# Seven-product projection of a second block: block sums through DRAM, roots inverted on 128x16, pooled rotation one group later

## The reference

```python
h = rms_norm(x, norm_w[l]) * (1.0 + scale[:, None, :]) + shift[:, None, :]
proj = jnp.einsum('bsd,de->bse', h, w_in[l])            # 1024 -> 2888
u_pool, g_pool, q, k, v, g_attn, qi, ki, wi = jnp.split(proj, split_points, axis=-1)
pool_out = pool_mixer(u_pool, w_pool[l], pool_scale[l]) * jax.nn.silu(g_pool)
q = rope(rms_norm(q.reshape(B, S, N_HEADS, HEAD_DIM), q_norm_w[l]), pos)
k = rope(rms_norm(k.reshape(B, S, N_KV_HEADS, HEAD_DIM), k_norm_w[l]), pos)
qi = rope(qi.reshape(B, S, N_IDX_HEADS, IDX_DIM), pos)
```

## Time and profile before

| what | value |
|---|---|
| median of 3 runs | 3106.57 us (3103.05 to 3109.3) |
| the profiled execution's own time | 3103.51 us |
| its span in the trace | 3101.7 us |
| mean granted clock of PE | 0.977 of full speed |
| busy, share of the span | PE 94%, DVE 78%, ACT 56%, POOL 17% |
| out_b, 1599 to 1738 us | 139 us, PE busy 121.8 |
| rotate, 1738 to 2248 us | 510 us, 24 groups |

### The profile page before, as it was taken

One profiled execution on the slowest core, in us unless ns is written; L12 is line 12 of the kernel. 1 busy time (PEld: TensorE's weight loads), 2 busy tenths in 40 slices (PEclk: granted clock), 3 DMA queues, 4 the chain that ended last, 5 costly groups with the idle time before them and its releaser, 6 DMA issues. The chain is left out here.

```text
span 3101.7 us, 49546 instructions
## 1 busy us (share of the span) xinstructions
PE 2916.2 (94%) x17248; PEld 2326.3 (75%) x17248; DVE 2428.9 (78%) x3533; ACT 1746.5 (56%) x3207; POOL 522.3 (17%) x791
## 2 busy tenths in 40 slices
PE   6999999999999999999998898899977899999899
PEld 5888888888878886777777677677755677777687
DVE  8888887766676758889878799799768898888553
ACT  5343422232454537777767654555478899888510
POOL 2000000000000001000114333343212333243100
PEclk8999999999999999999999999999989999999999
DMA  4434422257755433111135544544471111111774
GB/s 123 124 106 128 153 68 68 68 184 258 220 153 168 144 114 102 36 37 39 46 99 192 169 150 129 171 126 155 143 146 45 25 32 28 26 39 39 166 220 140
DMA packets 414557, 355.22 MB, mean 115 GB/s; under 512 B 100738, under 2 KB 362882, under 8 KB 411876
## 3 DMA queue, kind: packets, MB, share of 16 engines
q1 hardware_dynamic: 412500, 347.79, 38.2%
q0 software_dynamic: 1088, 3.93, 0.7%
q10 hardware_dynamic: 720, 0.31, 0.1%
HBM read 229.13 MB, written 112.87 MB: 110 GB/s over the span
## 5 line engine op out<-in xcount | busy, mean ns | idle before, releaser
L349 ACT ACTIVATE s_mx_w_hi<-s_mx_raw 128x512 fp32r<-128x512 f32 x224 | 138.5, 628 | 310.3 <-PE p_oa_acc L705 238.0
L705 PE MATMUL p_oa_acc<-s_h_a_hi,s_mx_w_hi 128*128 128x512 f32 x744 | 291.4, 392 | 8.8 <-DVE s_h_a_lo L448 7.1
L705 PE MATMUL p_oa_acc<-s_h_a_hi,s_mx_w_lo 128*128 128x512 f32 x744 | 290.3, 390 | 0.0
L705 PE MATMUL p_oa_acc<-s_h_a_lo,s_mx_w_hi 128*128 128x512 f32 x744 | 290.2, 390 | 0.0
L2151 PE MATMUL p_pr_ps<-s_pr_x_hi,s_pr_w_hi 128*128 128x512 f32 x588 | 233.1, 396 | 13.9 <-DVE s_pr_w_lo L2116 9.0
L1825 DVE TENSOR_TENSOR_SCAN s_st_prod<-s_st_soft,s_st_prod 128x512 f32<-128x512 f32 x192 | 234.8, 1269 | 8.2 <-ACT s_st_soft L1752 7.5
L2151 PE MATMUL p_pr_ps<-s_pr_x_lo,s_pr_w_hi 128*128 128x512 f32 x588 | 231.2, 393 | 0.0
L2151 PE MATMUL p_pr_ps<-s_pr_x_hi,s_pr_w_lo 128*128 128x512 f32 x588 | 231.0, 393 | 0.0
L1752 ACT ACTIVATE s_st_soft<-p_st_z 128x512 f32<-128x512 f32 (+3 forms) x320 | 153.4, 533 | 108.5 <-PE p_st_z L1878 107.7
L4243 PE MATMUL p_sa_turn<-s_ident,s_sa_arg 128*128 128x128 f32 x1088 | 164.8, 287 | 42.3 <-ACT s_sa_prob L3841 23.0
L491 DVE TENSOR_TENSOR s_mx_w_lo<-s_mx_raw,s_mx_w_hi 128x512 fp32r<-128x512 f32 x224 | 153.3, 685 | 53.6 <-ACT s_mx_w_hi L349 52.1
(11 more groups left out here) (489 smaller groups left out, 7890.3 us busy)
## 6 DMA issues: line engine op xcount, KB each, us to landing
s_mx_raw<-in_w_in_a SPq DMA_DIRECT2D x128, 256.0 KB, 3.8
s_pb_ada<-in_w_ada SPq DMA_DIRECT2D x16, 768.0 KB, 7.2
s_pr_w_a<-in_w_in SPq DMA_DIRECT2D x44, 256.0 KB, 3.2
s_pr_w_raw<-in_w_in SPq DMA_DIRECT2D x44, 256.0 KB, 3.3
d_rot_hi<-s_pr_rot SPq DMA_DIRECT2D x18, 512.0 KB, 2.7
d_y_t<-s_mx_y SPq DMA_DIRECT2D x16, 512.0 KB, 5.4
s_oa_y_raw<-d_y_t SPq DMA_DIRECT2D x16, 512.0 KB, 6.9
s_oa_x<-in_x SPq DMA_DIRECT2D x16, 512.0 KB, 4.9
```

What stands on the lines that cost most here:

```text
L705: ins = nc.tensor.matmul(bank, w[:, m, k, :], a[:, m, k, :], start=(k == 0 and n == 0), stop=(k == KH - 1 and n == 2))
```

## The change

1. **Block sums.** `sum` leaves rotate. In project, at steps 8 to 14, SP loads the raw blocks of the 11 groups that have them (`load_blocks`, four of 256 KB each), POOL makes the four sums (`sum_blocks`, 44 operations), and SP stores them to DRAM one step later (`store_blocks`, `d_w_sums`). rotate then loads seven blocks per group where it loaded four, each straight to the place of its low part, for both halves of the sequence.
2. **Roots.** The four reciprocals of 128x256 are replaced: the 64 rows of a head hold the same root, so two DMAs gather one row of each head into 128x16 (`gather_roots`), one reciprocal inverts that, a DMA stores 8 KB to DRAM and two broadcast it to 128x1024 (`spread_inverse`). `times_inverse`, `low_turned`, `take_high` and the stores of a norm group come one group later.
3. **Pooled turn.** The index query of a pool group is multiplied, added, split and stored one group later, in the group after the next norm group's first half; `mix` moves from behind the fourth product to behind the fifth.
4. **finish** (128x512) goes from POOL to DVE, ahead of `leave_c`.
5. **out_b.** The 14 gates go from POOL to DVE; the pieces of the factor are made one per step from 9 to 16, then 2, 1, 2, 1; the first whole group waits for the pieces of its own product only; two of the four last `store_late` go ahead of the A12 load.

The core of the diff (declarations, space and argument changes left out):

```diff
+    def load_blocks(self, sp, w_in, n):
+        j, of = n % 2, column_groups(0)[1 + n]
+        if n >= 2:
+            sp.wait_ge(self.blocks_out[j], 64 * (n // 2))
...
+    def store_blocks(self, sp, w_sums, n):
+        sp.wait_ge(self.blocks_summed, 4 * n + 4)
...
+    BLOCKS_AT = {8: (0, 1), 9: (2,), 10: (3, 4), 11: (5,), 12: (6, 7), 13: (8,), 14: (9, 10)}
...
+            for n in BLOCKS_AT.get(g - 1, ()):
+                proj.store_blocks(sp, w_sums, n)
+            for n in BLOCKS_AT.get(g, ()):
+                sp.wait_ge(late_lo, AHEAD)
+                proj.load_blocks(sp, w_next, n)
         next_space.load_first(sp, out_t, (upper_out, 16 * END), product, MULTS * END)
...
-    PIECES_AT = {9: 2, 10: 2, 11: 1, 12: 1, 13: 2, 14: 2, 15: 2, 16: 1, 17: 1}
+    PIECES_AT = {**{step: 1 for step in range(9, 17)}, 17: 2, 18: 1, 19: 2, 20: 1}
...
+        def gather_roots(g):
+            sp.wait_ge(rooted, norms_to(g) + 1)
...
+                sp.dma_start(roots[rows], wide[h * HD:h * HD + 1].rearrange("o (c n) -> o c n", n=pairs.ROOTS)).then_inc(roots_in, 16)
+        def store_inverse(g):
+            sp.wait_ge(roots_inverted, norms_to(g) + 1)
...
+            sp.dma_start(inverse_row.rearrange("h (c n) -> (h c) n", n=pairs.ROOTS), roots[:]).then_inc(inverse_out, 16)
+        def spread_inverse(g):
+            sp.wait_ge(inverse_out, 16 * (norms_to(g) + 1))
...
+                sp.dma_start(inverse[h * HD:h * HD + HD], inverse_row[h].partition_broadcast(HD)).then_inc(inverse_in, 16)
...
     def gpsimd(pool):
-        for g in range(1, N):
...
-                for n in range(3):
-                    pairs.sum(nc, pool, nxt, n)
-            if kinds[g] != "tail":
-                finish(g)
...
+        late_difference()
...
     def scalar(act):
+            norm, pool = older(g, "norm"), older(g, "pool")
...
+            if pool is not None:
+                take_high(pool)
+            if more and g:
+                pairs.split_hi(nc, act, nxt, S.A11_B11)
             if whole:
                 keep_u2(g)
...
-                if q == S.A12_B21 and kinds[was] == "pool":
+                if q == S.S3_T3 and kinds[was] == "pool":
                     mix(was)
```

More of the change, by code:

```diff
@@ L2741, in sync @@
                 load_late_half(0)
-            if g and kinds[was] != "gates":
+            if was_kind in ("norm", "tail"):
                 swap(was)
-            if nxt < N and nxt > 1 and kinds[nxt] != "tail":
-                for which in ("a21", "a22", "a11"):
-                    pairs.load(sp, nxt, which)
-            if g and kinds[was] == "tail":
+            if kinds[g] != "tail" and was_kind != "tail":
+                pairs.load(sp, g, S.A22_T4)
+            if more:
+                pairs.load(sp, nxt, S.A11_B11)
@@ L2748, in sync @@
+            if norm is not None:
+                store_rot(norm)
+            if was_kind == "tail":
                 store_tail(was)
-            if g and kinds[was] == "norm":
+            if was_kind == "norm":
                 store_plain(was, True, lower_out[was % 2])
-            if g and kinds[was] == "gates":
+            if was_kind == "gates":
                 store_plain(was, False, upper_out[was % 2])
                 store_plain(was, True, lower_out[was % 2])
+            if more:
+                pairs.load(sp, nxt, S.S1_T1)
@@ L2754, in sync @@
+            if norm is not None:
+                store_low(norm)
+            if was_kind == "norm":
+                gather_roots(was)
+            if pool is not None:
+                store_rot(pool)
+            if more:
+                pairs.load(sp, nxt, S.S2_T2)
+            if pool is not None:
+                store_low(pool)
+            if was_kind == "norm":
+                store_inverse(was)
             if g == LAST:
                 load_late_half(1)
-            if nxt < N and nxt > 1:
-                if kinds[nxt] == "tail":
-                    for h in range(2):
-                        pairs.load_tail(sp, nxt, h)
-                else:
-                    pairs.load(sp, nxt, "a12")
@@ L2762, in sync @@
-            if g and kinds[was] == "pool":
+                for h in range(2):
+                    pairs.load_tail(sp, nxt, h)
+            if more:
+                pairs.load(sp, nxt, S.A12_B21)
+            if was_kind == "norm":
+                spread_inverse(was)
+            if more:
+                pairs.load(sp, nxt, S.S3_T3)
+            if was_kind == "pool":
                 store_pooled(was)
-            if g and kinds[was] != "gates":
+                swap(was)
+            if was_kind == "tail":
@@ L2765, in sync @@
                 store_rot(was)
                 store_low(was)
+            if more:
+                pairs.load(sp, nxt, S.S4_B22)
+                if kinds[g] == "tail":
+                    pairs.load(sp, nxt, S.A22_T4)
             if g == N - 2:
@@ L2999, in scalar @@
                 late_high(2)
-            if was_kind == "norm":
-                take_high(was)
             if kinds[g] == "norm":
@@ L3219, in vector @@
                 late_low(0)
-            if more and g:
-                pairs.split_lo(nc, dve, nxt, S.S1_T1)
-            if was_kind == "norm":
-                invert(was, 3)
-                times_inverse(was)
-            if more and g:
-                pairs.split_lo(nc, dve, nxt, S.A11_B11)
-            if was_kind in ("pool", "tail"):
+            if more:
+                pairs.split_lo(nc, dve, nxt, S.S2_T2)
+            if was_kind == "tail":
                 low_turned(was)
```

362 lines of the change are left out of this document (183 added, 179 removed).

## The result

The changed kernel takes 3112.57 us (median of 12 runs, 3108.53 to 3119.61), the kernel before, run beside it, 3105.67 (12 runs, 3101.83 to 3112.42). The ratio is 1.0025, with a 95% interval of 1.0016 to 1.0033: a little **slower**, where 3076 was forecast. The profiled execution of the changed kernel took 3109.64, its span is 3107.6, so 5.9 over the span of before.

A forecast was written before the change was run, and what follows sets the result against it. PE sets rotate's pace, and most of its idleness is DVE's lateness, with DVE slowed beside POOL. Terms 11 + 8 + 10 + 3 - 2 = +30 us gave 3073.5, or 3076 on the median's footing; 8-in-10 range 3048 to 3102.

The forecast's parts named there:

- The bottleneck: In rotate, PE sets the pace and DVE, slowed beside POOL's sums, is late; 34.8 us lost in sixteen groups.
- the sixteen groups: Groups of norm and pool in rotate: 347.1 us instead of 358.25, gain +11, bounds +35 and -4.
- The odd groups: Eight rotate groups after a pool group: 20.8 us each, 166.4 together, 0.35 each over their floor.
- Out_b: Thirteen tiles before the tail: half of 15.5 lost us taken back, +8, bounds 0 and 13.
- the tail and first groups: Tail and first two groups, 69.4 us with 53.1 of work: gain +10, bounds 3 and 15.
- the middle: Four groups with the tail, 85.7 us, 1966.09 to 2051.75: gain +3, bounds 0 and 8.
- the stall at S3_T3: Eight groups after a norm group: PE waits for `keep_u2`, at least 1.4 us, taken as 2.0 each; 180.7 together.
- the 0.6 for the clock: Average loss from the lower clock after each S3_T3 stall in the eight groups after a norm group.
- Rival two: S3_T3 stall is 3 us with 1.5 for the lower clock each time: 195.9 for eight groups, 3091; chance 0.15.
- DVE's schedule: After a norm group: six operations end at 7.78 us, three more for the pool tile at 11.2; `keep_u2` done at 13.2.
- The ends, "-2": SP's queue at project's end and later stores at rotate's end cost 2 us, bounds 0 and -6.
- Rival three: Roots' store lands in 8.8 us, not 2.7, holding SP's queue: 3.3 lost in ten pairs, 3109; chance 0.09.

The follow-up runs named there:

- experiment 6: Kernel before with POOL's four sums per group replaced by memsets; only the rotation is read: last group starts at 2195.20 instead of 2229.37 us.
- experiment 8: Kernel before with parts 1 and 5, loads in order of products, A22 split later: 3077.62 us, ratio 0.9907.
- experiment 2: Changed kernel with A22's low part behind the older pool tile's three operations on DVE: 3106.49 us.
- experiment 3: Changed kernel with SP reordered: next phase's first loads before the last two block-sum stores, last group's plain stores before the norm tile's: 3116.26 us.
- experiment 1: Changed kernel with `keep_u2` ahead of the older pool tile's copy and A11's copy on ACT: 3112.00 us, ratio 1.0016.
- experiment 5: experiment 1 with the next group's loads ahead of pool-tile stores and the roots' store and spread on SP: 3095.11 us, ratio 0.9961.
- experiment 11: experiment 8, `mix` behind fifth product, `split_pooled` behind `keep_u2`; A11's low part, and in first half's last group A22's load and `keep_u3`, earlier: 3068.96 us, ratio 0.9875.

## Why the prediction was wrong

**The bottleneck and what its removal is worth: right.** DVE's lateness beside POOL held PE. With the sums gone and the orders kept the last group starts 32 us earlier (experiment 6), and the program with the sums from DRAM takes 3077.6 (experiment 8). That this lies next to the 3076 that was forecast for the whole change is chance: there the sixteen groups give 25.0 us where the forecast has 11, and the other stretches take 15.0 back. Low parts of 687 ns, `mix` at 2.1 us of waiting and PE at 80.00 in project came as forecast. The odd groups' sum of 166.4 us is the forecast's to the digit by luck: seven groups stand at 20.45 to 20.69, near their floor, and one, with the widest window of the first half, takes 22.77. Out_b gave 6.1 for 8, the tail and first groups 6.3 for 10, the middle 2.3 for 3, each inside its bounds.

**The step that failed is the stall at S3_T3, "8 x (19.99 + 2.0 + 0.6) = 180.7".** The place, the engine, the cause and the count were right; both sizes were not. The eight groups took 201.6, 25.2 each: the stall of 2.0 was 2.82 to 4.15 us, 3.24 in the mean, and the 0.6 for the clock was 1.97 (1.7 to 3.1 in seven groups; 0.3 in the one behind whose stall the granted clock stayed at 1.00). In the stretch from 1855.0 to 1858.5 the granted clock was 0.63. So the sixteen groups lost 10 us where 11 were to be gained, below the term's lower bound of -4; of the 36 us by which the forecast missed in the profiled executions, 21 are here. Rival two named 3 us and 1.5, and even that was short. Two things were missing from DVE's schedule, which I had taken from a group without a gate. The squares start at 2.45 us, not at 1.78, behind the table load. And A22's load, which in the kernel before was made a group earlier, is now issued behind the swaps of the same group, so that its low part holds cos back to 6.73 us; experiment 2 measured that piece, 12.8 us of the eight groups. With both, the pool tile's sum ends at 12.8 instead of 11.2, and `keep_u2` at 14.9 instead of 13.2. In the two groups without a gate the squares did start at 1.78, and the late loads of S4's sum and of A22 did the harm: the pool tile's sum ended at 13.9 and 14.0.

**The ends, "-2":** +2.3 ahead of out_b and +4.6 behind the last group, over the bound of 6. The queue order that I named explains a quarter of it at most (experiment 3). The cause of the 4.0 us within the selection, whose instructions are the same, stays open; over all these kernels but experiment 6, that stretch takes 847 to 855 us.

**Rival three** did not decide the time: in the changed kernel the spread was issued 1.6 to 3.2 us after the roots' store, as with the 2.7 that I took, and the odd groups paid nothing. But the mechanism is real, by other waits than the one it named. With `keep_u2` ahead (experiment 1) SP's queue takes the stall's place, at `keep_u3` and at `mix`, and with the loads moved ahead (experiment 5) the store's landing, then up to 4.5 us, and the spread's behind it hold DVE.

**What it comes to.** Parts 1 and 5 together give -29 us, part 4 nothing or a loss of a few, and parts 2 and 3, roots inverted through DRAM and tiles finished one group later, cost 30 to 35 as ordered; with the two orders of experiments 1 and 5, 17 of them come back. Reciprocals were worth 5 to 9 us by themselves, and in experiments 6, 8 and 11 the even groups stand at their floor with all of them. How the loss divides between parts 2 and 3, and the gain between parts 1 and 5, was not tried apart, nor were the small transfers tried on another queue than SP's.

## What to carry to other kernels

An engine that is busy 91% is worth relieving only where something waits for it: of two removals here, 52 us of DVE's own reciprocals gave 5 to 9 us, and 146 us of sums on POOL, for which PE waits in no row, gave some 30. In the best kernel (experiment 11) DVE is again busy 91.0 of the 100 us from 1800 on, and PE all of them. When a change also re-orders, lay out the new schedule for the worst group with every load's issue time in it, and ask what the in-order engine holds behind each new wait; a copy that empties a bank for PE belongs ahead of any copy that waits for a long chain. Try the parts apart: the gain of one can be hidden whole under the price of the others, as 29 us were here.

## What the runs showed of the hardware

POOL's memsets did not slow DVE: in experiment 6 POOL was still busy (16.7 of 100 us between 1800 and 1900), with low parts at 697 ns, against 687 in the changed kernel, where POOL stands still there. With POOL's sums, which read two operands, their mean was 917. In project, where the sums went, DVE's instructions in the window from 1040 to 1120 have a mean of 0.80 us (64.76 of 81) instead of 0.64 (48.72 of 76). The largest case is a single one in experiment 11, where POOL's subtraction of 128x2048 runs beside DVE's of the same shape:

```profile
1955.68 4.59 POOL L2821 TENSOR_TENSOR s_pr_x_raw<-s_pr_ahead,s_pr_ahead 128x2048 f32<-128x2048 f32 x1
```

```profile
1956.57 5.84 DVE L3153 TENSOR_TENSOR s_pr_x_raw<-s_pr_ahead,s_pr_x_raw 128x2048 f32<-128x2048 f32 x1 [4.84 <-DMA s_pr_x_raw<-d_rows_late]
1962.51 2.29 DVE L3158 TENSOR_TENSOR s_pr_x_raw<-s_pr_ahead,s_pr_x_raw 128x2048 f32<-128x2048 f32 x1
```

DVE's took 5.84 us there and 2.29 right after: it lost 3.55 of the 3.70 us in which both ran. In this kernel that loss is on DVE's way to the low parts of the late factors, behind which PE stands for 11.3 us ahead of the tail. The Trainium skill ("SBUF — State Buffer", section "Who interferes with whom") says that a DVE instruction with two SBUF inputs contends with a GpSimd instruction that reads SBUF, not with one that only writes it, and calls the port pair that they share an exclusive lock. Both traces agree: 697 ns beside memsets, and 3.55 of 3.70 us lost beside a subtraction.
